# Convolution states and taps turned on the tensor engine, and an attention bias laid out by query in DRAM

## The chip, the cores and the metric

One core of a Trainium2 chip runs the whole kernel in one launch. The metric is the device time of one execution in microseconds (us). Three executions of the kernel before took 2809.85, 2809.88 and 2812.94 us; the median is 2809.88 us.

## The reference, cut to what matters

One layer of a streaming encoder is applied to 2048 prompt rows and 64 sample rows (2112 in all). Input LayerNorm is followed by one input projection, whose columns feed three head groups; their outputs go through an output projection, a LayerNorm, a convolutional feed-forward network and a last LayerNorm. Two pieces of it are touched here.

```
# band attention, per head: 128 queries see up to 640 keys
rel = arange(CHUNK)[:, None] + A_PAST_ROWS - arange(A_BAND)[None, :]
s = s + table[:, clip(rel, -63, 128) + 63]      # bias depends on query - key alone
# depthwise causal convolution of width 4 on the 896 x/B/C features
y = b + w[0]*xp[:, 0:L] + w[1]*xp[:, 1:1+L] + w[2]*xp[:, 2:2+L] + w[3]*xp[:, 3:3+L]
state_out = xp[:, L:]                            # last 3 rows, (3, 896), an output
```

The prompt starts from a zero state and the sample from `state_ssm_conv` (3, 896). Both end states are outputs: `prompt_ssm_conv` and `sample_ssm_conv`, each (3, 896). All numbers are float32; large products are made of three products of rounded high and low parts.

## The kernel before, in words

The kernel is seven stages, one after the other: `project_rows`, `project_features`, `attention`, `ssd_and_gmlp`, `mix_out`, `ffn_up`, `ffn_down`. A stage ends only when all its engines and all its stores are done, and the next one then begins on all engines together. Intermediate results pass through DRAM. Inside a stage each engine has its own instruction stream, and semaphores order them.

`project_features` (L375 to L667) computes q and k (6 tiles of 128 features) and the convolution's input (7 tiles, `NXBC`) with features on the partitions. It goes over the rows in seven groups of 304 (the last has 288); `step(g, p, i)` is one group, with 13 tiles j. TensorE (PE) writes tile j to PSUM bank j % 8; before tile j it waits until the tile four places before has been taken out (`evac_done`, L660). In the first group, eight tiles are accumulated side by side as the weights arrive. ScalarE (ACT) takes out q and k tiles (L544), after waiting for the store of the tile two before it in the same buffer; after the sixth it rounds the next group's input (`split_hi`, L536); then it takes out the convolution tiles (L566) and applies SiLU (L556). VectorE (DVE) makes the low parts (L600, L587) and the convolution (L613 to L631): `taps` and `shift` hold the filter with features on the partitions, `halo` and `halo_smp` the last three columns of the prompt and of the sample. SyncE (SP) loads weights (L453, L454) and issues the stores of q, k (L462, L463) and of the convolution (L467).

GpSimd (POOL) first issues eight loads (L487 to L491) for `taps`, `shift` and `halo_smp`. They turn (c, 896) rows into [128, 7] columns by moving one 4-byte element at a time. POOL then loads the second group's input (L484), spreads the bias table over 768 columns in `ext` on 6 partitions, stores it as `rel_ext` (L505), waits for that store, and only then loads the third group's input. At the end of the stage, SP stores the states with six more DMAs of 4-byte elements (L472, L474), and the stage waits for them (L475).

`attention` (L700 to L1048) starts with a load of `bias_up` on SP (L774), which reads `rel_ext` with overlapping rows, so that partition r holds the row that starts at column r. This is the bias with its query rows in reverse order. PE therefore multiplies it with a flipped identity, 12 matmuls in all (L962, L963), ACT copies the six results to `bias` (L939), and POOL writes the mask to two corners (L820, L821) and then issues eight loads of the key cache (L824) and three copies (L826 to L828). On SP, the load of the bias is followed by seven loads each for tiles 0 and 1 (L784, L787, L789) and, once all six heads of the tile before have been scored, for every later tile. Per head, PE computes scores (L979, L980), DVE adds the bias and takes the maximum (L861), ACT takes the exponential (L924), PE turns the result (L994) and multiplies with V (L1012). A tile is 128 queries, six heads; tile t sees min(t + 1, 5) blocks of keys.

```
sp.wait_ge(conv_done, NXBC * (NG + 1))                      # L470
for c in range(3):                                          # L471, again at L473 for the sample
    sp.dma_start(d["prompt_ssm_conv"][c].rearrange("(m p) -> p m", p=P), halo[:, :, c], ...)
pool.dma_start(d["rel_ext"], ext[:]).then_inc(ext_stored, 16)   # L505
pool.wait_ge(ext_stored, 16)                                    # L506
```

Of the kernel before, what the change touches and what calls it, by code (L numbers as in the profile page):

```python
# [33 lines left out]
HEADS = 6  # L34
# [340 lines left out]
def project_features(nc, d):  # L375
    with nc.cleanup_on_exit(), ExitStack() as ctx:
# [14 lines left out]
        halo, halo_smp = m.sb("halo", [P, NXBC, 3]), m.sb("halo_smp", [P, NXBC, 3])  # L391
        taps, shift = m.sb("taps", [P, NXBC, 4]), m.sb("shift", [P, NXBC])
        ext = m.sb("ext", [HEADS, WIN + P])
        ps_y = m.ps("ps_y", [P, 8, 512])
# [3 lines left out]
        small_loaded, halo_zeroed = m.sem("small_loaded"), m.sem("halo_zeroed")  # L398
# [43 lines left out]
        with nc.Block() as block:  # L442
            @block.sync
            def _(sp):
# [25 lines left out]
                sp.wait_ge(conv_done, NXBC * (NG + 1))  # L470
                for c in range(3):  # L471
                    sp.dma_start(d["prompt_ssm_conv"][c].rearrange("(m p) -> p m", p=P), halo[:, :, c], allow_slow_non_contiguous=True).then_inc(state_stored, 16)  # L472
                for c in range(3):  # L473
                    sp.dma_start(d["sample_ssm_conv"][c].rearrange("(m p) -> p m", p=P), halo_smp[:, :, c], allow_slow_non_contiguous=True).then_inc(state_stored, 16)  # L474
                sp.wait_ge(state_stored, 16 * 6)  # L475
# [5 lines left out]
            def _(pool):  # L481
# [4 lines left out]
                for c in range(4):  # L486
                    pool.dma_start(taps[:, :, c], d["ssm_conv_w"][c].rearrange("(m p) -> p m", p=P),  # L487
                                   allow_slow_non_contiguous=True).then_inc(small_loaded, 16)
                pool.dma_start(shift[:], d["ssm_conv_b"].rearrange("(m p) -> p m", p=P), allow_slow_non_contiguous=True).then_inc(small_loaded, 16)
                for c in range(3):  # L490
                    pool.dma_start(halo_smp[:, :, c], d["state_ssm_conv"][c].rearrange("(m p) -> p m", p=P),  # L491
                                   allow_slow_non_contiguous=True).then_inc(small_loaded, 16)
# [12 lines left out]
                pool.dma_start(d["rel_ext"], ext[:]).then_inc(ext_stored, 16)  # L505
# [16 lines left out]
            def _(act):  # L522
# [47 lines left out]
                groups(act, step)  # L570

            @block.vector
            def _(dve):
                for k in range(KD):
# [15 lines left out]
                dve.wait_ge(small_loaded, 128)  # L590
                dve.wait_ge(halo_zeroed, 1)

                def step(g, p, i):
# [11 lines left out]
                    for j in range(NXBC):  # L605
# [5 lines left out]
                        if tail(g):  # L611
                            dve.tensor_copy(c[:, TAIL + 3:TAIL + 6], halo_smp[:, j, :])
                        dve.tensor_copy(c[:, 0:3], halo[:, j, :]).then_inc(halo_in_done, 1)  # L613
# [5 lines left out]
                        dve.tensor_scalar(y, c[:, 0:nc_], taps[:, j, 0:1], shift[:, j:j + 1], ALU.mult,  # L619
                                          ALU.add).then_inc(tap_done, 1)  # L620
                        for e in (1, 2):
                            dve.wait_ge(tap_done, 3 * u + e)
                            dve.scalar_tensor_tensor(out=y, in0=c[:, e:e + nc_], scalar=taps[:, j, e:e + 1], in1=y,
                                                     op0=ALU.mult, op1=ALU.add).then_inc(tap_done, 1)
                        if tail(g):
                            dve.tensor_copy(halo_smp[:, j, :], c[:, n + 3:n + 6])
                            dve.tensor_copy(halo[:, j, :], c[:, TAIL:TAIL + 3])
                        else:
                            dve.tensor_copy(halo[:, j, :], c[:, n:n + 3])
                        dve.wait_ge(tap_done, 3 * u + 3)  # L630
                        dve.scalar_tensor_tensor(out=y, in0=c[:, 3:3 + nc_], scalar=taps[:, j, 3:4], in1=y,  # L631
# [4 lines left out]
            def _(pe):  # L636
                def step(g, p, i):
# [12 lines left out]
                    if first:  # L650

                        for k in range(KD):
# [3 lines left out]
                            for j in range(8):  # L656
                                product(j, k)
# [9 lines left out]
                groups(pe, step)  # L667

# [31 lines left out]
def attention(nc, d):  # L700


    with nc.cleanup_on_exit(), ExitStack() as ctx:
# [4 lines left out]
        bias, bias_up = m.sb("bias", [P, HEADS, WIN]), m.sb("bias_up", [P, HEADS, WIN])  # L708
        ident, flip, ident_r = m.sb("ident", [P, P]), m.sb("flip", [P, P]), m.sb("ident_r", [P, HD], F32R)
# [13 lines left out]
        flip_done, bias_flipped, bias_copied = m.sem("flip_done"), m.sem("bias_flipped"), m.sem("bias_copied")  # L723
# [45 lines left out]
        with nc.Block() as block:  # L769
            @block.sync  # L770
            def _(sp):

                toeplitz = bass.AP(d["rel_ext"].tensor, 0, [[1, P], [WIN + P, HEADS], [1, WIN]])
                sp.dma_start(bias_up[:], toeplitz).then_inc(bias_loaded, 16)  # L774
# [37 lines left out]
            def _(pool):  # L812
                make_identity(pool, ident, zero_done, ident_done)
                pool.memset(flip[:], 0.0).then_inc(zero_done, 1)
                pool.wait_ge(zero_done, 2)
                pool.affine_select(out=flip[:], in_=flip[:], compare_op=ALU.not_equal, fill=1.0, base=1 - P,
                                   pattern=[[1, P]], channel_multiplier=1).then_inc(flip_done, 1)

                pool.wait_ge(bias_copied, HEADS)
# [99 lines left out]
            def _(act):  # L919
# [17 lines left out]
                for h in range(HEADS):  # L937
                    act.wait_ge(bias_flipped, h + 1)
# [1648 lines left out]
```

## Time and profile before

| what | value |
|---|---|
| median of three runs | 2809.88 us |
| the profiled execution: its own time | 2820.15 us |
| the profiled execution: span of its instructions | 2818.7 us |
| mean granted clock of PE over the span | 0.957 of 2.4 GHz |
| busy: PE, DVE, ACT, POOL | 2577.7, 1638.2, 1053.8, 168.8 us |
| `project_features` | 291.7 to about 642 us of the span |
| `attention` | 642.5 to about 914 us of the span |

The profile is one execution. Its own time is 1.45 us above its span, and 10.27 us above the median of the runs. All positions below are microseconds from the start of its span. "Granted clock" is the share of the full 2.4 GHz that PE was given: 1.00, or 0.50 (1.2 GHz). The DMA share is the mean busy share of the 16 DMA engines; it can exceed 1 where transfers overlap. A landing time runs from the issue's start until the last byte has arrived. An entry like `[9.57 <-DMA at_v<-v_rows]` says how long the engine had been idle before this instruction, and what ended that.

### The profile page before, as it was taken

To read this page: it belongs to the slowest core of one execution; us is meant where nothing else is said; L and a number is where in the kernel's file an instruction comes from. 1 tells how busy PE (TensorE), PEld (TensorE's weight loads), DVE (VectorE), ACT (ScalarE), POOL (GpSimd) and SP (SyncE) were. 2 spreads that over 40 slices of the span, in tenths; PEclk is the share of its full clock that TensorE was granted. 3 is DMA by queue.
4 is the path that set the end of the run, shared out by engine and by line. 5 is a ranking of instruction groups with operands and counts; after the bars stand their busy time and mean duration, and the time that the engine had idled before them with its cause. 6 is when DMAs were issued, how large, how long until landed. Compare 5 with 4: busy or idle time off the path is not lost. (4 is left out here: it accounts for less than half of the span.)

```text
span 2818.7 us, 47061 instructions
## 1 busy us (share of the span) xinstructions
PE 2577.7 (91%) x15094; PEld 2363.7 (84%) x15094; DVE 1638.2 (58%) x3296; ACT 1053.8 (37%) x1996; POOL 168.8 (6%) x244
## 2 busy tenths in 40 slices
PE   6999799965998787995999989999999979999998
PEld 5888699964997776884899989999999967888885
DVE  5342445433775776665899986667766654333333
ACT  4444322214663113222555554445555442111110
POOL 0000100001000570110000000000000000000000
PEclk9999899987997898997999999999999989999999
DMA  5443623157441545444777779777788744322321
GB/s 198 137 156 118 207 97 101 66 50 176 118 126 38 169 140 199 161 159 155 256 245 245 243 252 292 257 258 250 239 257 255 245 165 145 94 77 78 93 78 52
DMA packets 418766, 468.52 MB, mean 166 GB/s; under 512 B 45309, under 2 KB 352389, under 8 KB 418651
## 3 DMA queue, kind: packets, MB, share of 16 engines
q1 hardware_dynamic: 405210, 418.50, 48.5%
q0 software_dynamic: 13456, 48.76, 5.2%
q8 instruction: 55, 0.90, 0.1%
q14 instruction: 45, 0.36, 0.0%
HBM read 312.51 MB, written 155.60 MB: 166 GB/s over the span
## 5 line engine op out<-in xcount | busy, mean ns | idle before, releaser
L2265 PE MATMUL fu_ps_a<-fu_x_hi,fu_w 128*128 128x354 f32 (+1 forms) x1056 | 348.2, 330 | 45.3 <-ACT fu_part L2042 16.9
L2267 PE MATMUL fu_ps_a<-fu_x_hi,fu_w 128*128 128x354 f32 (+1 forms) x1056 | 346.4, 328 | 0.0
L2266 PE MATMUL fu_ps_a<-fu_x_lo,fu_w 128*128 128x354 f32 (+1 forms) x1056 | 345.8, 328 | 0.0
L107 PE MATMUL fd_ps_y<-fd_w_hi,fd_h_hi 128*128 128x512 f32 (+1 forms) x748 | 292.5, 391 | 17.6 <-DVE fd_h_lo L2454 17.6
L108 PE MATMUL fd_ps_y<-fd_w_lo,fd_h_hi 128*128 128x512 f32 (+1 forms) x748 | 291.9, 390 | 0.0
L109 PE MATMUL fd_ps_y<-fd_w_hi,fd_h_lo 128*128 128x512 f32 (+1 forms) x748 | 291.6, 390 | 0.0
L2454 DVE TENSOR_TENSOR fd_h_lo<-fd_h_raw,fd_h_hi 128x256 fp32r<-128x256 f32 (+1 forms) x187 | 77.7, 417 | 311.6 <-ACT fd_h_hi L2426 311.6
L2265 PEld LDWEIGHTS fu_ps_a<-fu_x_hi,fu_w 128*128 128x128 f32 x1056 | 201.1, 190 | 53.5 <-ACT fu_part L2042 18.0
L107 PE MATMUL pf_ps_y<-pf_xt_hi,pf_w_hi 128*128 128x304 f32 (+1 forms) x728 | 221.2, 304 | 20.8 <-DVE pf_xt_lo L581 18.7
L2426 ACT CAST fd_h_hi<-fd_h_raw 128x256 fp32r<-128x256 f32 (+1 forms) x187 | 74.7, 401 | 404.8 <-PE fd_ps_y L109 394.2
L109 PE MATMUL pf_ps_y<-pf_xt_hi,pf_w_lo 128*128 128x304 f32 (+1 forms) x728 | 220.9, 303 | 0.0
L108 PE MATMUL pf_ps_y<-pf_xt_lo,pf_w_hi 128*128 128x304 f32 (+1 forms) x728 | 219.9, 302 | 0.0
L2266 PEld LDWEIGHTS fu_ps_a<-fu_x_lo,fu_w 128*128 128x128 f32 x1056 | 201.5, 191 | 0.0
L2267 PEld LDWEIGHTS fu_ps_a<-fu_x_hi,fu_w 128*128 128x128 f32 x1056 | 201.1, 190 | 0.0
L107 PEld LDWEIGHTS fd_ps_y<-fd_w_hi,fd_h_hi 128*128 128x128 f32 (+1 forms) x748 | 138.5, 185 | 51.2 <-DVE fd_w_lo L2492 16.8
L2265 PE MATMUL fu_ps_c<-fu_x_hi,fu_w 128*128 128x354 f32 (+1 forms) x528 | 174.5, 331 | 6.0 <-ACT fu_part L2061 6.0
L2266 PE MATMUL fu_ps_c<-fu_x_lo,fu_w 128*128 128x354 f32 (+1 forms) x528 | 173.3, 328 | 0.0
L2267 PE MATMUL fu_ps_c<-fu_x_hi,fu_w 128*128 128x354 f32 (+1 forms) x528 | 172.6, 327 | 0.0
L109 PEld LDWEIGHTS fd_ps_y<-fd_w_hi,fd_h_lo 128*128 128x128 f32 (+1 forms) x748 | 138.4, 185 | 32.0
L108 PEld LDWEIGHTS fd_ps_y<-fd_w_lo,fd_h_hi 128*128 128x128 f32 (+1 forms) x748 | 138.5, 185 | 31.6
L107 PEld LDWEIGHTS pf_ps_y<-pf_xt_hi,pf_w_hi 128*128 128x128 f32 x728 | 138.5, 190 | 21.4 <-DVE pf_xt_lo L581 18.9
L107 PE MATMUL pr_ps_y<-pr_w_hi,pr_xt_hi 128*128 128x512 f32 (+3 forms) x408 | 148.8, 365 | 4.7 <-DVE pr_xt_lo L306 4.7
(318 smaller groups left out, 5803.6 us busy)
## 6 DMA issues: line engine op xcount, KB each, us to landing
fu_w<-fu_w_split SPq DMA_DIRECT2D x176, 512.0 KB, 4.4
fu_w_raw<-ffn_w_in SPq DMA_DIRECT2D x132, 512.0 KB, 5.5
fu_w_split<-fu_w SPq DMA_DIRECT2D x44, 1024.0 KB, 4.6
fd_h_raw<-h_t SPq DMA_DIRECT2D x176, 128.0 KB, 2.2
h_t<-fu_val SPq DMA_DIRECT2D x88, 176.0 KB, 1.9
fd_raw<-ffn_w_out SPq DMA_DIRECT2D x22, 512.0 KB, 4.7
x_rows<-pr_xr SPq DMA_DIRECT2D x16, 512.0 KB, 2.8
xt<-pr_xt SPq DMA_DIRECT2D x16, 512.0 KB, 4.0
```

Source lines behind the costliest of these rows:

```text
L107: pe.matmul(out, lhs_hi, rhs_hi, start=first, stop=False)
L108: pe.matmul(out, lhs_hi, rhs_lo, start=False, stop=False)
L109: return pe.matmul(out, lhs_lo, rhs_hi, start=False, stop=last)
L2265: pe.matmul(out, wh, xh, start=first and k == 0, stop=False, skip_group_check=True)
L2266: pe.matmul(out, wh, xl, start=False, stop=False, skip_group_check=True)
L2267: last = pe.matmul(out, wl, xh, start=False, stop=k == KH - 1, skip_group_check=True)
L2426: act.copy(h_hi[:, x.slot, :, :x.n], h_raw[:, x.slot, :, :x.n]).then_inc(h_hi_done, 1)
L2454: dve.tensor_tensor(h_lo[:, x.slot, :, :x.n], h_raw[:, x.slot, :, :x.n], h_hi[:, x.slot, :, :x.n].bitcast(F32), ALU.subtract).then_inc(h_l ...
```

## The change

The eight small loads at the start of `project_features` become three, of contiguous 512-byte rows, into `vec_rows` (56 rows of 128); PE turns them in one transpose into PSUM bank 7, and DVE copies the result to `vecs` after the first low part. The six stores of the states become two PE transposes, two ACT copies and two stores of 21 rows of 512 bytes. `ext` is no longer stored once: POOL stores it 128 times over, shifted by one column each time, as `bias_rows` (6, 128, 640), 1920 KB, and still waits for this store. In `attention` ACT issues one load of `bias`, already in the right order, 768 rows of 2560 bytes; the flipped identity, the twelve matmuls and the six copies are gone. The layouts of `taps` and `halo` change with this.

```
 # project_features
+        ident, vec_rows, vecs = m.sb("ident", [P, P]), m.sb("vec_rows", [NV, P]), m.sb("vecs", [P, 8, NXBC])
+        taps, shift, halo_smp = vecs[:, 0:4], vecs[:, 4], vecs[:, 5:8]
+        halo, states_t = m.sb("halo", [P, 3, NXBC]), m.sb("states_t", [3 * NXBC, 2, P])
+        d["bias_rows"] = nc.dram_tensor("pf_bias_rows", (HEADS, P, WIN), F32, kind="Internal").ap()
...
 # SP
-                sp.wait_ge(conv_done, NXBC * (NG + 1))
-                for c in range(3):
-                    sp.dma_start(d["prompt_ssm_conv"][c]..., halo[:, :, c], ...).then_inc(state_stored, 16)
-                for c in range(3):
-                    sp.dma_start(d["sample_ssm_conv"][c]..., halo_smp[:, :, c], ...).then_inc(state_stored, 16)
-                sp.wait_ge(state_stored, 16 * 6)
+                sp.wait_ge(states_done, 2)
+                sp.dma_start(d["prompt_ssm_conv"].rearrange("c (m p) -> (c m) p", p=P), states_t[:, 0, :]).then_inc(state_stored, 16)
+                sp.dma_start(d["sample_ssm_conv"].rearrange("c (m p) -> (c m) p", p=P), states_t[:, 1, :]).then_inc(state_stored, 16)
+                sp.wait_ge(state_stored, 32)
 # POOL
-                for c in range(4): pool.dma_start(taps[:, :, c], ...)
-                pool.dma_start(shift[:], ...)
-                for c in range(3): pool.dma_start(halo_smp[:, :, c], ...)
+                pool.dma_start(vec_rows[0:4 * NXBC, :], ...).then_inc(vec_loaded, 16)
+                pool.dma_start(vec_rows[4 * NXBC:5 * NXBC, :], ...).then_inc(vec_loaded, 16)
+                pool.dma_start(vec_rows[5 * NXBC:, :], ...).then_inc(vec_loaded, 16)
+                make_identity(pool, ident, zero_done, ident_done)
...
-                pool.dma_start(d["rel_ext"], ext[:]).then_inc(ext_stored, 16)
+                by_query = bass.AP(ext[:].tensor, ext[:].offset + P - 1, [list(ext[:].ap[0]), [-1, P], [1, WIN]])
+                pool.dma_start(d["bias_rows"], by_query).then_inc(ext_stored, 16)
                 pool.wait_ge(ext_stored, 16)
 # ACT, after the last group
+                act.wait_ge(states_turned, 1)
+                for e in range(2):
+                    act.copy(states_t[:, e, :], ps_y[0:3 * NXBC, 7, e * P:(e + 1) * P]).then_inc(states_done, 1)
 # DVE, after the first low parts
+                    if k == 0:
+                        dve.wait_ge(vec_turned, 1)
+                        dve.tensor_copy(vecs[:].rearrange("p a b -> p (a b)"), ps_y[:, 7, 0:NV]).then_inc(vec_done, 1)
 # PE, before the first group, before tile 7 of it, and after the last group
+                pe.wait_ge(ident_done, 1)
+                pe.wait_ge(vec_loaded, 48)
+                pe.transpose(ps_y[:, 7, 0:NV], vec_rows[:], ident[0:NV, 0:NV]).then_inc(vec_turned, 1)
...
+                                if k == 0 and j == 7:
+                                    pe.wait_ge(vec_done, 1)
...
+                pe.wait_ge(conv_done, NXBC * (NG + 1))
+                for e, rows in enumerate((halo[:]..., halo_smp...)):
+                    last = pe.transpose(ps_y[0:3 * NXBC, 7, e * P:(e + 1) * P], rows, ident[:])
+                last.then_inc(states_turned, 1)
 # attention: SP, POOL, ACT, PE
-                toeplitz = bass.AP(d["rel_ext"].tensor, 0, [[1, P], [WIN + P, HEADS], [1, WIN]])
-                sp.dma_start(bias_up[:], toeplitz).then_inc(bias_loaded, 16)
-                pool.memset(flip[:], 0.0) ... pool.affine_select(out=flip[:], ...)
-                pool.wait_ge(bias_copied, HEADS)
+                pool.wait_ge(ident_done, 1)
+                pool.wait_ge(bias_loaded, 16)
                 pool.memset(bias[0:64, :, WIN - 64:], MASKED)
                 pool.memset(bias[64:P, :, 0:64], MASKED).then_inc(bias_done, 1)
-                for h in range(HEADS):
-                    act.wait_ge(bias_flipped, h + 1)
-                    act.copy(bias[:, h, :], (ps_s[:, 0] if h % 2 == 0 else ps_t)[:, 0:WIN]).then_inc(bias_copied, 1)
+                act.dma_start(bias[:], d["bias_rows"].rearrange("h p c -> p h c")).then_inc(bias_loaded, 16)
-                pe.wait_ge(flip_done, 1)
-                pe.wait_ge(bias_loaded, 16)
-                for h in range(HEADS):
-                    ...
-                    pe.matmul(dst[:, 0:512], flip[:], bias_up[:, h, 0:512], start=True, stop=True)
-                    pe.matmul(dst[:, 512:WIN], flip[:], bias_up[:, h, 512:], start=True, stop=True).then_inc(bias_flipped, 1)
-                pe.wait_ge(bias_copied, HEADS)
```

## Rows read from the trace of the kernel before

**Rows 1.** the page: busy time and share of each engine over the span.

```profile
PE 2577.7 (91%) x15094; PEld 2363.7 (84%) x15094; DVE 1638.2 (58%) x3296; ACT 1053.8 (37%) x1996; POOL 168.8 (6%) x244
```

**Rows 2.** the stretch view; columns: sum, engines, granted clock, DMA share, GB/s.

```profile
620.00:630.00 10.00, 0.00 (x0) 0.00 (x0) 0.00 (x0) 0.00 (x0) 0.00 (x0) 0.50 1.96 1
```

**Rows 3.** the timeline from the last convolution to the first attention instructions.

```profile
612.70 0.52 DVE L631 SCALAR_TENSOR_TENSOR pf_conv<-pf_cin,pf_taps,pf_conv 128x291 f32<-128x291 f32 x1
616.06 4.59 SPq L474 DMA_DIRECT2D sample_ssm_conv<-pf_halo_smp  x3
...
642.54 0.37 SPq L774 DMA_DIRECT2D at_bias_up<-rel_ext  x1
```

**Rows 4.** the view by tile, pf_halo_smp: issues, and time to landing.

```profile
L474 SPq DMA_DIRECT2D sample_ssm_conv<-pf_halo_smp x3: 563/567/3371, 616.1 to 617.3; - x3
...
DMA to landing us min/median/max: 6.6/13.4/24.2
```

**Rows 5.** nearest rows for the operations that are new (three views).

```profile
L994 PE MATMUL at_ps_t<-at_ident,at_s x450: 216/273/435, 662.8 to 898.9; 128*128 128x128 f32 x140, 64*128 64x64 f32 x8, 64*64 64x64 f32 x2
...
607.33 0.22 ACT L564 COPY pf_cin<-pf_ps_y 128x64 f32<-128x64 f32 x1
...
dt_rows<-pr_dt_out SPq DMA_DIRECT2D x16, 3.0 KB, 1.6
```

**Rows 6.** the timeline at the start of attention.

```profile
650.44 1.12 SPq L789 DMA_DIRECT2D at_v<-v_rows  x1
...
660.64 0.33 PE L979 MATMUL at_ps_s<-at_k_hi,at_q 128*128 128x128 f32 x1 [0.78 <-ACT at_bias L939]
...
661.69 0.29 DVE L861 CUSTOM_DVE_ANT_0 at_s<-at_ps_s,at_bias 128x128 f32<-128x128 f32 x1 [18.27 <-POOL at_bias L821]
...
681.76 0.69 PE L979 MATMUL at_ps_s<-at_k_hi,at_q 128*128 128x384 f32 x1 [9.57 <-DMA at_v<-v_rows]
```

**Rows 7.** landing times: the bias load; V of tile 0; V of all tiles (L789).

```profile
at_bias_up<-rel_ext SPq DMA_DIRECT2D x1, 1920.0 KB, 8.4
...
DMA to landing us min/median/max: 6.4/6.4/6.4
...
DMA to landing us min/median/max: 2.7/4.0/12.5
```

**Rows 8.** the stretch view at the start of attention (columns as in Rows 2).

```profile
651.00:652.00 1.00, 0.91 (x1) 0.50 (x2) 0.00 (x0) 0.00 (x0) 0.00 (x0) 0.50 1.23 227
662.00:663.00 1.00, 0.68 (x5) 0.54 (x5) 0.91 (x7) 0.79 (x4) 1.00 (x2) 1.00 0.00 0
```

**Rows 9.** the start of the projection: the small loads, the first split and product.

```profile
L487 POOL DMA_DIRECT2D pf_taps<-ssm_conv_w x4: 982/990/1023, 292.2 to 295.2; - x4
...
299.00 1.21 ACT L529 CAST pf_xt_hi<-pf_xt 128x1216 fp32r<-128x1216 f32 x1 [1.38 <-DMA pf_xt<-xt]
...
301.72 0.62 PE L107 MATMUL pf_ps_y<-pf_xt_hi,pf_w_hi 128*128 128x304 f32 x1 [18.69 <-DVE pf_xt_lo L581]
```

**Rows 10.** the stretch view there.

```profile
300.00:306.00 6.00, 4.28 (x17) 4.29 (x18) 1.77 (x2) 1.78 (x2) 0.24 (x2) 0.50 1.00 234
306.00:316.00 10.00, 10.00 (x69) 9.88 (x69) 7.21 (x5) 5.91 (x5) 0.00 (x0) 0.95 1.04 395
```

**Rows 11.** around the table's store: POOL, ACT, and two DMAs' landings.

```profile
331.14 0.54 POOL L505 DMA_DIRECT2D rel_ext<-pf_ext  x1 [0.30 <-POOL pf_ext L503]
...
335.17 0.42 ACT L544 ACTIVATE pf_qk_hi<-pf_ps_y 128x304 fp32r<-128x304 f32 x1 [1.92 <-DMA qk_lo<-pf_qk_lo]
...
DMA to landing us min/median/max: 5.8/6.3/6.7
...
pf_xt<-xt POOLq DMA_DIRECT2D x5, 1216.0 KB, 7.0
```

**Rows 12.** ACT in the second group of the projection.

```profile
372.27 2.22 ACT L536 CAST pf_xt_hi<-pf_xt 128x2432 fp32r<-128x2432 f32 x1
...
388.64 0.41 ACT L566 COPY pf_cin<-pf_ps_y 128x304 f32<-128x304 f32 x1 [1.98 <-PE pf_ps_y L109]
```

More of the change, by code:

```diff
@@ L484, in load_xt @@
                     pool.dma_start(xt[:, p, :, :n], d["xt"][:, :, gcols(g)]).then_inc(xt_loaded[p], 16)
[L486 to L492, printed above, removed]
+                pool.dma_start(vec_rows[0:4 * NXBC, :], d["ssm_conv_w"].rearrange("c (m p) -> (c m) p", p=P)).then_inc(vec_loaded, 16)
+                pool.dma_start(vec_rows[4 * NXBC:5 * NXBC, :], d["ssm_conv_b"].rearrange("(m p) -> m p", p=P)).then_inc(vec_loaded, 16)
+                pool.dma_start(vec_rows[5 * NXBC:, :], d["state_ssm_conv"].rearrange("c (m p) -> (c m) p", p=P)).then_inc(vec_loaded, 16)
+                make_identity(pool, ident, zero_done, ident_done)
                 pool.memset(halo[:], 0.0).then_inc(halo_zeroed, 1)
@@ L588, in split_lo @@
                                       ALU.subtract).then_inc(xt_lo_done, 1)
-                dve.wait_ge(small_loaded, 128)
+                dve.wait_ge(vec_done, 1)
                 dve.wait_ge(halo_zeroed, 1)
@@ L622, in step @@
                             dve.wait_ge(tap_done, 3 * u + e)
-                            dve.scalar_tensor_tensor(out=y, in0=c[:, e:e + nc_], scalar=taps[:, j, e:e + 1], in1=y,
+                            dve.scalar_tensor_tensor(out=y, in0=c[:, e:e + nc_], scalar=taps[:, e, j:j + 1], in1=y,
                                                      op0=ALU.mult, op1=ALU.add).then_inc(tap_done, 1)
                         if tail(g):
-                            dve.tensor_copy(halo_smp[:, j, :], c[:, n + 3:n + 6])
-                            dve.tensor_copy(halo[:, j, :], c[:, TAIL:TAIL + 3])
+                            dve.tensor_copy(halo_smp[:, :, j], c[:, n + 3:n + 6])
+                            dve.tensor_copy(halo[:, :, j], c[:, TAIL:TAIL + 3])
                         else:
-                            dve.tensor_copy(halo[:, j, :], c[:, n:n + 3])
+                            dve.tensor_copy(halo[:, :, j], c[:, n:n + 3])
                         dve.wait_ge(tap_done, 3 * u + 3)
-                        dve.scalar_tensor_tensor(out=y, in0=c[:, 3:3 + nc_], scalar=taps[:, j, 3:4], in1=y,
+                        dve.scalar_tensor_tensor(out=y, in0=c[:, 3:3 + nc_], scalar=taps[:, 3, j:j + 1], in1=y,
                                                  op0=ALU.mult, op1=ALU.add).then_inc(conv_done, 1)
@@ L667, in _ @@
                 groups(pe, step)
+                pe.wait_ge(conv_done, NXBC * (NG + 1))
+                for e, rows in enumerate((halo[:].rearrange("p a b -> p (a b)"), halo_smp.rearrange("p a b -> p (a b)"))):
+                    last = pe.transpose(ps_y[0:3 * NXBC, 7, e * P:(e + 1) * P], rows, ident[:])
+                last.then_inc(states_turned, 1)
 class Band:
@@ L707, in attention @@
         cache = m.sb("cache", [P, 4, HEADS, 2, HD])
-        bias, bias_up = m.sb("bias", [P, HEADS, WIN]), m.sb("bias_up", [P, HEADS, WIN])
-        ident, flip, ident_r = m.sb("ident", [P, P]), m.sb("flip", [P, P]), m.sb("ident_r", [P, HD], F32R)
+        bias = m.sb("bias", [P, HEADS, WIN])
+        ident, ident_r = m.sb("ident", [P, P]), m.sb("ident_r", [P, HD], F32R)
         s = m.sb("s", [P, 3, WIN])
```

22 lines of the change are left out of this document (7 added, 15 removed).

## The prediction

> **What bounds the kernel now.** I read the page first: PE is busy in 91% of the span [rows 1], so a change elsewhere counts only where PE has nothing to do. The stretch view shows such a place: from 620 to 630 us no engine works, the DMA engines show a share of 1.96 and move 1 GB/s [rows 2]. The timeline says what that is. The last convolution starts at 612.70 and takes 0.52 us; then SP issues six stores of 4-byte elements, and the next stage starts at 642.54 [rows 3]. The view by tile gives the last of these: issued at 617.3, it lands up to 24.2 us later, at 641.5 [rows 4]. So 29.3 us lie between the last convolution (613.2) and attention, and the next stage starts 1.05 us after that landing. The third place is attention's own start. PE's first score starts at 660.64 after a wait for the copies of the turned bias, the first bias is added at 661.69, and later PE stands 9.57 us, until 681.76, for the values of tile 2 [rows 6]. I call attention's start S (642.54 now). The last two places are in the projection: its first product at 301.72 waits for a chain that begins with the input's landing at 299.0 [rows 9], and PE meets late stores near 335 [rows 11].
>
> **The change part by part.**
>
> 1. *States at the end of the projection.* Removed are six stores and their landing. Added, one after the other: two turns on PE, at 0.27 us each and at most 0.44 [rows 5], about 0.6 us with their start; two ACT copies of 128 columns, a little over the 0.22 us for 64 columns [rows 5], 0.5 us; two issues on SP of some 0.5 us, and the landing, 1.6 us for the smallest store [rows 5]. That is 613.2 + 0.1 + 0.6 + 0.1 + 0.5 + 0.1 + 0.6 (the second issue starts) + 1.8 = 617.0; with a margin for the waits 617.4, and S comes 1.05 later, at 618.4. Gain 24.1 us; bounds 21 (each store lands in 5 us) and 25. PE has just come out of full clock, so its two turns may run at half clock; the 0.44 covers that.
>
> 2. *Filter and states at the start.* POOL issues three loads of 56 rows instead of eight of 7168 elements, each of which occupied it for 0.98 us or more [rows 9]. From 300 to 306 us the DMA engines were as busy as later (1.00 against 1.04) but moved 234 GB/s against 395 [rows 10]; the small loads are what differs. The first weights and half of the input must land before ACT can start at 299.00 [rows 9]: at the higher rate some 1.3 us earlier, after which ACT's own first cast is in the way. Against it PE now waits for the three loads and a turn. The last of them is issued near 294.3 and lands 2 to 6 us later, and the turn (0.3 to 0.44) lies before the first split is ready at about 300.3 or just behind it. DVE's copy (0.2 us) falls in its idle time, and PE needs it only at the eighth tile, some 5 us in. POOL's identity, 0.5 us, is behind its loads and ahead of nothing that is late. I take a gain of 1.0; bounds a loss of 1 and a gain of 1.5.
>
> 3. *The table's store.* POOL's store at 331.14 [rows 11] grows from 18 KB to 1920 KB, in 768 rows of 2560 bytes read from 6 partitions, and POOL still waits for it. No row shows such a store. The nearest is the load of the same 768 rows on 128 partitions, which lands in 8.4 us [rows 7]. If six engines carry it at the share that one of 16 had there (1920 KB in some 6.4 us is 19 KB per us and engine), 320 KB each take 17 us, so 18 to 19 with landing. I take 18 us. It hits two things. First, the stores of q and k tiles in flight at 333 to 340. Beside the next input's load these landed in 5.8 to 6.7 us, and ACT waited for such a store at 335.17 already [rows 11]. Now the ones before them are late as well, by 3 to 4 us, of which PE (four banks ahead) passes on about 2; with the late convolution stores after it I count 3.5. Second, the third group's input is loaded after it, 7.0 us [rows 11]. In the second group ACT splits that input at 372.27 (2.22 us) and cannot take out a convolution tile before; PE's twelfth tile needs that one and would start when the eleventh is done, at 388.6 [rows 12]. So the store may take 388.6 - 331.1 - 7.3 - 2.6 = 47 us before PE waits, and each us beyond costs one. At 18 it costs nothing. Loss 3.5; bounds 1 and 12.
>
> 4. *The bias in attention.* SP's own load goes (0.4 us), ACT issues the new one, and POOL's flip, PE's 12 matmuls and ACT's six copies go, a chain of about 9 us behind the bias's landing. Yet the time does not fall by that. Tile 0's V was issued at 650.44 and landed 6.4 us later [rows 6, 7], at S + 14.3, and tile 1's loads were behind it; the DMA engines ran at 1.23 with 225 GB/s in that stretch and only at 662 stood still [rows 8]. The same 1920 KB and the same tiles must still come in. So the first score moves from S + 18.1 to about S + 14, a gain of 4 there, and the next wait is again for loads: POOL's cache loads, behind the mask, start at about S + 11 instead of S + 18.9 and now meet tile 1's loads. What sets the end is tile 2's V, which landed at S + 39.2 (681.76) [rows 6]. Its loads are preceded by the same bytes and gain only the DMA engines' idle time at 662 and their weaker stretch after it, in all 2 to 3.5 us. I take 3.0; bounds 0 and 5, and a loss of 3 if the order turns bad. PE idles and cools before tile 2 either way. Afterwards nothing in attention or behind it is touched.
>
> *Sum*, against the profiled execution's 2820.15 us: 24.1 + 1.0 - 3.5 + 3.0 = 24.6, so 2795.5 us. The median of the runs lies 10.27 us below that execution, so the forecast is 2785.3 us.
>
> **The rivals.**
>
> *A, the table's store is far slower* (about 50 us instead of 18), because six partitions cannot be read as fast as 128. For it: 1920 KB come out of 6 partitions; against it: nothing measured. The third group's input then comes 3 us too late, and for some 45 us every store of the projection that shares an engine with it lands late, another 5 us beyond my 3.5. Gain 24.6 - 8 = 16.6: 2793.3 us.
>
> The Trainium skill (SBUF — State Buffer, section "Door 1: The DMA port swizzle") puts partitions 0 to 3 on one port of some 27 GB/s; four of the six rows of `ext` would then take about 48 us. No row of this trace reads so much from so few partitions, so none shows it.
>
> *B, attention gives nothing back*: the early cache loads (eight on POOL) delay tiles 1 and 2, and tile 2's values land 1 us later after S than now. For it: landing rose from a median of 4.0 to 12.5 us when they met tile 2's loads [rows 7]. Gain 24.1 + 1.0 - 3.5 - 1 = 20.6: 2789.3 us.
>
> *C, slower than before.* The table's store runs through one engine. At 19 KB per us it takes about 100 us; the third group's input, the split and the convolution copy behind it come 53 us after PE's eleventh tile: 24.6 - 53 is a loss of 28.4, 2838.3 us. It breaks even at 47 + 24.6 = 72 us of store, and is measurably slower from 78. Against it: the bias load of as many rows was spread over the engines [rows 7, 8].
>
> *D, the states are not what the stage waits for.* Then S would hardly move and only parts 2 to 4 count, about 2809 us. Against it: no other transfer is in flight, 1 GB/s is moved, and the next stage follows the last landing by 1.05 us [rows 2 to 4].
>
> **How the numbers follow.** Forecast 0.50, A 0.28, B 0.13, C 0.04, D 0.02, and 0.03 for a store between A and C that about cancels the gain. The range starts at 2779, where part 1 gives 25, part 2 1.5, part 3 costs 1 and part 4 gives 5 (2779.4), and reaches through B and A, with A's own spread, to 2797. A measurement of this kernel can tell 0.2% (5.6 us) from no change: above 2815.5 is only C (0.04), within lie D and half of the last case (0.04), and faster holds 0.92.
>
> **What would show it.** In the profile after: attention starts 5 us after the last convolution, not 29; both state stores land in about 2 us; PE's first projection product comes near 300.7; POOL's wait for the table's store (18 us, or 50) stands before its load of the third group's input; ACT's second split near 372 waits for DMA only in A and C; in attention the first score comes near S + 14 and the first of tile 2 near S + 36. The forecast is wrong if the table's store lasts over 47 us, if stores of the projection land in more than 8 us for long, or if tile 2 starts later than S + 39.

## The result, and the profile after

The changed kernel took 2832.17 us, median of four runs (2828.67 to 2835.51); the kernel before, beside it, 2810.02 us (2809.85 to 2812.94). The ratio is 1.0073, 95% interval 1.0054 to 1.0091: slower by 22 us, where 2785.3 us was forecast. The profiled execution of after has 2828.87 us of its own and a span of 2827.4 us. The last convolution now ends at 661.6 instead of 613.2. The whole loss arises before that point; what follows it is faster than before.

The page of after, busy time and share by engine, as in [rows 1]:

```profile
PE 2560.0 (91%) x15073; PEld 2350.3 (83%) x15073; DVE 1638.8 (58%) x3297; ACT 1049.4 (37%) x1992; POOL 163.2 (6%) x239
```

PE has 18 us less to do than before (for the most part the flips, and the stretch at half clock told of at the end), so the loss is idle time. The view of PE's waits names it. Its columns are who waits for what, total us, times, longest us; the window runs from the projection to attention's start.

```profile
PE pf_ps_y L107 <- ACT pf_qk_hi L545: 50.1, 1, 50.1
PE at_ps_s L979 <- DMA at_v<-v_rows: 17.5, 1, 17.5
PE pf_ps_y L646 <- DMA pf_vec_rows<-state_ssm_conv: 15.4, 1, 15.4
PE pf_ps_y L683 <- DVE pf_conv L638: 3.1, 1, 3.1
```

50.1 us stand in one wait of the projection, for ACT's take-out of a q/k tile; before, this wait was 2.1 us. It is new, and it is the first thing to follow back. The timeline from 326 to 381 us, of POOL, then ACT, then PE:

```profile
326.40 1.10 POOL L506 DMA_DIRECT2D pf_bias_rows<-pf_ext  x1 [0.30 <-POOL pf_ext L503]
385.37 0.93 POOL L487 DMA_DIRECT2D pf_xt<-xt  x1 [57.88 <-DMA pf_bias_rows<-pf_ext]
...
363.95 0.42 ACT L545 ACTIVATE pf_qk_hi<-pf_ps_y 128x304 fp32r<-128x304 f32 x1 [35.27 <-DMA qk_lo<-pf_qk_lo]
380.37 0.42 ACT L545 ACTIVATE pf_qk_hi<-pf_ps_y 128x304 fp32r<-128x304 f32 x1 [15.99 <-DMA qk_lo<-pf_qk_lo]
...
380.84 0.62 PE L107 MATMUL pf_ps_y<-pf_xt_hi,pf_w_hi 128*128 128x304 f32 x1 [50.15 <-ACT pf_qk_hi L545]
```

The landing times of the table's store and of the new bias load:

```profile
pf_bias_rows<-pf_ext POOLq DMA_DIRECT2D x1, 1920.0 KB, 58.4
at_bias<-pf_bias_rows ACTq DMA_DIRECT2D x1, 1920.0 KB, 9.0
```

POOL's store lasts 58.4 us, not 18. ACT needs a free `qk_lo` buffer for the next tile and stands 35.27 and then 15.99 us for SP's stores of the tiles before. The view by tile of `pf_qk_lo` from 326 to 390 us has those stores:

```profile
L468 SPq DMA_DIRECT2D qk_lo<-pf_qk_lo x6: 434/3204/6739, 329.4 to 387.4; - x6
...
DMA to landing us min/median/max: 4.0/13.3/38.8
```

They land in up to 38.8 us. In [rows 11] ACT waited 1.92 us for such a store. The stretch view (columns as in [rows 2]) says that this is no lack of bandwidth overall: from 340 to 380 us almost nothing computes, and the DMA engines move 40 to 61 GB/s at a share of 0.28 to 0.38. A share of 0.38 of 16 engines is six of them. Six rows of `ext` are being stored. Why the share is lower after 360 us is told with experiments 5 to 7.

```profile
300.00:306.00 6.00, 4.82 (x19) 4.82 (x20) 5.03 (x4) 3.17 (x2) 0.00 (x0) 0.50 1.04 398
340.00:360.00 20.00, 0.00 (x0) 0.00 (x0) 0.00 (x0) 0.00 (x0) 0.00 (x0) 0.50 0.38 61
360.00:380.00 20.00, 0.00 (x0) 0.00 (x0) 0.47 (x1) 0.42 (x1) 0.00 (x0) 0.50 0.28 40
```

The three other places. The end of the projection and attention's start, all engines, answering to [rows 3]:

```profile
661.11 0.52 DVE L638 SCALAR_TENSOR_TENSOR pf_conv<-pf_cin,pf_vecs,pf_conv 128x291 f32<-128x291 f32 x1
661.69 0.29 PE L683 MATMUL pf_ps_y<-pf_ident,pf_halo 128*21 128x128 f32 x1 [3.10 <-DVE pf_conv L638]
662.17 0.39 ACT L574 COPY pf_states_t<-pf_ps_y 21x128 f32<-21x128 f32 x2
662.72 0.37 SPq L476 DMA_DIRECT2D prompt_ssm_conv<-pf_states_t  x1
663.14 0.28 SPq L477 DMA_DIRECT2D sample_ssm_conv<-pf_states_t  x1
...
665.49 0.72 SPq L798 DMA_DIRECT2D at_q<-qk_hi  x1
```

From the end of the last convolution (661.63) to S (665.49) it is 3.86 us, not 29.3. PE's first score, and its next wait in attention, answering to [rows 6]:

```profile
679.57 0.45 PE L979 MATMUL at_ps_s<-at_k_hi,at_q 128*128 128x128 f32 x1 [17.48 <-DMA at_v<-v_rows]
695.08 0.58 PE L979 MATMUL at_ps_s<-at_k_hi,at_q 128*128 128x256 f32 x1 [9.98 <-DMA at_v<-v_rows]
```

The start of the projection, answering to [rows 9]:

```profile
297.89 1.89 DVE L580 TENSOR_TENSOR pf_w_lo<-pf_w_raw,pf_w_hi 128x1664 fp32r<-128x1664 f32 x1 [11.52 <-ACT pf_w_hi L526]
298.57 0.32 PE L646 MATMUL pf_ps_y<-pf_ident,pf_vec_rows 56*128 56x56 f32 x1 [15.42 <-DMA pf_vec_rows<-state_ssm_conv]
299.70 1.42 DVE L585 TENSOR_TENSOR pf_xt_lo<-pf_xt,pf_xt_hi 128x1216 fp32r<-128x1216 f32 x1
301.18 0.29 PEld L107 LDWEIGHTS pf_ps_y<-pf_xt_hi,pf_w_hi 128*128 128x128 f32 x1 [2.46 <-DVE pf_xt_lo L585]
```

### The profile page after: what moved, and what is told of

Read it like the earlier page. It is cut to its first block and busy times, and to the rows that moved or that the text cites. A ratio compares the mean times of both kernels' runs of the same rounds, so it can differ in the third digit from the quotient of the medians.

```text
span 2827.4 us, 47008 instructions
## 1 busy us (share of the span) xinstructions
PE 2560.0 (91%) x15073; PEld 2350.3 (83%) x15073; DVE 1638.8 (58%) x3297; ACT 1049.4 (37%) x1992; POOL 163.2 (6%) x239
## 3 DMA queue, kind: packets, MB, share of 16 engines
q0 software_dynamic: 14304, 50.71, 5.8%
## 5 line engine op out<-in xcount | busy, mean ns | idle before, releaser
L107 PE MATMUL pf_ps_y<-pf_xt_hi,pf_w_hi 128*128 128x304 f32 (+1 forms) x728 | 221.9, 305 | 52.4 <-ACT pf_qk_hi L545 50.1
```

The lines of the kernel that those rows point to most:

```text
L107: pe.matmul(out, lhs_hi, rhs_hi, start=first, stop=False)
```

## The experiments

Fifteen kernels were run. "Ratio" is against the kernel before on the same chip, whose median was between 2812.8 and 2817.9 us there, with the 95% interval. S is attention's start in the profile.

**1. The states alone, with the filter.** The change's projection, but the 18 KB store of the table and attention as before.

```diff
-                pool.dma_start(d["bias_rows"], by_query).then_inc(ext_stored, 16)
+                pool.dma_start(d["rel_ext"], ext[:]).then_inc(ext_stored, 16)
```

> The states and the filter are turned on PE as in the change; the table's store (18 KB) and the whole attention are those of before. Theory 1 (the stored table costs about 50 us, the states and the filter give about 25): 2810 - 25.5 - 0.5 = about 2784 us, attention starts 4 us after the last convolution, no PE wait beyond 2.2 us in the projection's first group. Rival (the states' gain is taken back by attention's start, where the loads then are late): 2795 us or more.

Measured: 2791.29 us, ratio 0.9918 (0.9894 to 0.9942). S came at 619.8, not 642.5. So parts 1 and 2 together keep about what they promised, and the loss is in the table's store. The time is above the expected 2784 us, though, and one wait is longer than the 2.2 us expected. POOL, ACT and PE near 330 us in this kernel:

```profile
328.55 0.94 POOL L487 DMA_DIRECT2D pf_xt<-xt  x1 [2.01 <-DMA rel_ext<-pf_ext]
...
335.00 0.42 ACT L544 ACTIVATE pf_qk_hi<-pf_ps_y 128x304 fp32r<-128x304 f32 x1 [4.47 <-DMA qk_lo<-pf_qk_lo]
335.48 0.62 PE L107 MATMUL pf_ps_y<-pf_xt_hi,pf_w_hi 128*128 128x304 f32 x1 [5.98 <-ACT pf_qk_hi L544]
```

**2. The bias alone.** The kernel before with the large store, and the change's attention.

```diff
-                pool.dma_start(d["rel_ext"], ext[:]).then_inc(ext_stored, 16)
+                pool.dma_start(d["bias_rows"], by_query).then_inc(ext_stored, 16)
```

> The bias by query alone: the projection stores 1920 KB from 6 partitions and attention loads it, while states and filter move in 4-byte elements as before. Theory 1: the change's 2829 to 2835 us plus the 26 us of the states and the filter, 2855 to 2861 us. Rival (the turn on PE at the start or the new layout of the halo has a share in the loss): less than 2850 us.

Measured: 2856.94 us, ratio 1.0147 (1.0116 to 1.0178). The store lands in 58.4 us again, and PE waits 42.5 us for ACT's q/k tiles. The loss belongs to this half of the change, whatever the other half does.

**3. Is it POOL's wait?** As after, but POOL does not wait for the store before it loads the third group's input.

```diff
                 pool.dma_start(d["bias_rows"], by_query).then_inc(ext_stored, 16)
-                pool.wait_ge(ext_stored, 16)
...
                 step(NG - 2, 0, NG // 2 - 1)
+                pool.wait_ge(ext_stored, 16)
```

> As the change, but GpSimd does not wait for the table's store before it loads the third group's input; it waits at the end of its stream. Theory 1 (the cost is that the q and k stores queue behind the table's rows on shared DMA engines): nothing gained, PE still waits 45 to 50 us in the first group, 2826 to 2836 us. Rival, the way in which the prediction thought that a slow store would cost (the third group's input comes late): the time falls by 10 us or more.

Measured: 2836.24 us, ratio 1.0061 (1.0042 to 1.0079). The input is issued 58 us earlier, and nothing is gained: ACT still waits 37.59 us for a store of `qk_lo`. POOL and ACT:

```profile
327.67 0.93 POOL L487 DMA_DIRECT2D pf_xt<-xt  x1
...
365.80 0.42 ACT L545 ACTIVATE pf_qk_hi<-pf_ps_y 128x304 fp32r<-128x304 f32 x1 [37.59 <-DMA qk_lo<-pf_qk_lo]
```

So the path over which I had let the store cost anything large, the third group's input, carries none of it.

**4. Another place.** The same store, issued behind POOL's other work, at 470 us.

```diff
-                pool.dma_start(d["bias_rows"], by_query).then_inc(ext_stored, 16)
-                pool.wait_ge(ext_stored, 16)
...
                 step(NG - 2, 0, NG // 2 - 1)
+                pool.dma_start(d["bias_rows"], by_query).then_inc(ext_stored, 16)
+                pool.wait_ge(ext_stored, 16)
```

> As the change, but the same slow store of the table is issued at the end of GpSimd's stream, in the fifth or sixth group, where a q or k tile comes every 3.3 us. Theory 1: with two buffers per store each tile tolerates a landing of some 6 us, the table's rows make it 10 to 39 us, so PE still waits 30 to 50 us there: 2810 to 2835 us. Rival (only the first group is that tight, its eight tiles coming at once): 2790 us or less.

Measured: 2821.25 us, ratio 1.0011 (0.9997 to 1.0025), ten runs. The store still takes 58.6 us. These are PE's waits in the projection, of which one (5.4 us, at 337 us) lies in the first group, long before the store:

```profile
PE pf_ps_y L107 <- ACT pf_qk_hi L545: 17.7, 2, 12.3
PE pf_ps_y L107 <- ACT pf_cin L567: 11.3, 2, 8.2
```

So PE waits 23.6 us beside the store, in three waits, instead of 50.1; the expected 30 to 50 us were too much. ACT stands there for stores of the convolution (11.4, 9.8, 12.3, 9.5 and 6.6 us) more than for those of q and k. The place is worth some 17 us by the ratios; in neither place is the slow store free.

**5 to 7. Why the store is slow.** Three kernels change only where the table's rows are read from. Twice `ext` keeps its rows further apart (two and four partitions); once the 18 KB store is followed by a copy of 1920 KB from DRAM to DRAM, so that no partition is read.

```diff
-        ext = m.sb("ext", [HEADS, WIN + P])
+        ext = m.sb("ext", [4 * HEADS, WIN + P])      # the rows used: 0, 4, ..., 20
...
-                by_query = bass.AP(..., [list(ext[:].ap[0]), [-1, P], [1, WIN]])
+                by_query = bass.AP(..., [[4 * ext[:].ap[0][0], HEADS], [-1, P], [1, WIN]])
```

```diff
+                by_query = bass.AP(d["rel_ext"].tensor, P - 1, [[WIN + P, HEADS], [-1, P], [1, WIN]])
+                pool.dma_start(d["bias_rows"], by_query).then_inc(ext_stored, 16)
```

> As the change, but the six rows of the table lie on partitions 0, 4, 8, 12, 16 and 20 instead of 0 to 5; the same bytes, rows and descriptors. Theory 1 (reading is slow because neighbouring partitions share one way out of SBUF): the store lands in about 15 to 20 us instead of 58, PE's wait in the first group falls from 50 to 5 to 12 us, the time to 2786 to 2796 us. Theory 2 (six engines carry it, whatever the source): 58 us and 2829 us or more, as the change.

> As the change, but the table's rows lie on partitions 0, 2, 4, 6, 8 and 10. In the change four rows lay in the first four partitions (58.4 us), with rows four apart one did (19.4 us). Theory 1: two rows share the way out of each four partitions, so the store takes about half of 58.4 us, 27 to 32 us, PE waits 18 to 27 us in the first group, and the time is 2798 to 2808 us. Rival (any distance is as good as four): 19 to 20 us and about 2793 us.

> As the change, but the 18 KB table is stored to DRAM first and the 1920 KB are then copied from there, in the same order by head, on the same queue and at the same place. Theory 1 (slow only because they come out of neighbouring partitions): 12 to 22 us instead of 58, and 2785 to 2797 us. Rival (the long store costs by its destination, or by the order of its rows): about 58 us and 2829 us or more.

Landing times of the 1920 KB, with rows four apart, two apart, and out of DRAM:

```profile
pf_bias_rows<-pf_ext POOLq DMA_DIRECT2D x1, 1920.0 KB, 19.4
```

```profile
pf_bias_rows<-pf_ext POOLq DMA_DIRECT2D x1, 1920.0 KB, 32.6
```

```profile
pf_bias_rows<-rel_ext POOLq DMA_DIRECT2D x1, 1920.0 KB, 19.2
```

| rows read from | store, us | PE's wait for q/k tiles, us | time, us | ratio |
|---|---|---|---|---|
| partitions 0 to 5 (after) | 58.4 | 50.1 | 2832.17 | 1.0073 (1.0054 to 1.0091) |
| 0, 2, ..., 10 | 32.6 | 24.5 | 2809.97 | 0.9964 (0.9951 to 0.9976) |
| 0, 4, ..., 20 | 19.4 | 13.1 | 2792.65 | 0.9923 (0.9901 to 0.9946) |
| DRAM | 19.2 | 8.1 | 2788.16 | 0.9905 (0.9874 to 0.9935) |

PE's wait in the third of these kernels:

```profile
PE pf_ps_y L107 <- ACT pf_qk_hi L548: 13.1, 1, 13.1
```

In the first three rows of the table nothing changes but the distance of the source rows (and that `ext` is cleared beforehand where they are apart), and the duration falls with the number of rows among four neighbouring partitions: four, two, one. With one it equals the copy that reads no partition, so there something else limits. PE's wait falls with it, and stays 6 to 11 us below the store's length. With the rows two apart the time is 2 us above the expected range, with the rows four apart the wait is 1 us above it.

The three durations alone would also fit groups of eight partitions roughly, in which six, four and two rows lie (58.4 us would then become 39 and 19). The stretch view of after speaks for groups of four:

```profile
351.00:357.00 6.00, 0.00 (x0) 0.00 (x0) 0.00 (x0) 0.00 (x0) 0.00 (x0) 0.50 0.39 60
357.00:363.00 6.00, 0.00 (x0) 0.00 (x0) 0.00 (x0) 0.00 (x0) 0.00 (x0) 0.50 0.25 30
372.00:378.00 6.00, 0.00 (x0) 0.00 (x0) 0.00 (x0) 0.00 (x0) 0.00 (x0) 0.50 0.24 27
```

Until 357 us six of the 16 DMA engines are busy (0.39), from then on four (0.25). 357 us is 31 us after the issue, about as long as the store with two rows in each group took (32.6): the two rows on partitions 4 and 5 are through, the four on partitions 0 to 3 are not. In the last stretch those four move 27 GB/s together.

**8. Fewer bytes.** `ext` is stored 16 times, shifted by eight columns (243 KB), and the bias comes in eight loads of 240 KB.

```diff
+                by_eight = bass.AP(..., ext[:].offset + P - 8, [list(ext[:].ap[0]), [-8, 16], [1, WIN + 7]])
+                pool.dma_start(d["bias_part"], by_eight).then_inc(ext_stored, 16)
...
+                for b in range(8):
+                    act.dma_start(bias[b:P:8], d["bias_part"][:, :, 7 - b:7 - b + WIN]...)
```

> As the change, but the table is stored 16 times instead of 128 times over (shifted by eight columns each time, 243 KB from the same 6 partitions), and attention loads the bias with eight DMAs of 240 KB on ACT's queue. Theory 1: the store lands in 58.4 / 8 = about 7 to 9 us, PE waits some 3 to 6 us in the first group, and the time is 2782 to 2788 us. A theory by which the store's bytes do not matter (something else in the projection costs the 50 us) leaves it near 2829 us. If eight issues make the bias late in attention, its first score comes later than S + 15.

Measured: 2796.79 us, ratio 0.9935 (0.9915 to 0.9956). The store takes 9.0 us, PE's wait for q/k tiles is 8.4 us, but the first score comes only at S + 18.4: eight issues stand in ACT's stream and the loads compete with tile 0's. That is 9 us above the expected range. It repairs the store and gives part of it back in attention; that the issues and the loads are what delays the score was not tested apart.

**9, 10. Parts 1 and 2 apart.** The end states alone turned on PE; then the filter and the start states alone. The rest is as before in both.

```diff
 # states alone: ident built as in the change; loads of taps, shift, halo_smp as before
+                    last = pe.transpose(ps_y[0:3 * NXBC, 7, e * P:(e + 1) * P], rows, ident[:])
 # filter alone: the six element-wise state stores as before
+                pe.transpose(ps_y[:, 7, 0:NV], vec_rows[:], ident[0:NV, 0:NV]).then_inc(vec_turned, 1)
```

> Only the end states are turned on PE; the filter comes in 4-byte elements and attention is that of before. Expected: attention starts 3.9 us after the last convolution instead of 29.3, so 25.4 us less, PE's wait in the first group stays at 2 us: ratio to before 0.991. If the gain is partly taken back by attention, the ratio is above 0.993.

> Only the filter and start states come as rows and are turned on PE; the end states are stored in 4-byte elements and attention is that of before. Theory (the weights then come earlier and take the third group's input load with them into the first q and k stores): PE's first product 0.5 to 1.1 us earlier, its wait in the first group 5 to 7 us against 2.1, the last convolution 2 to 4 us later, 0.1% slower than before. The prediction's part 2 said 1.0 us faster.

Measured: states alone 2789.40 us, ratio 0.9907 (0.9889 to 0.9926), S at 617.8. Filter alone 2818.72 us, ratio 1.0015 (1.0003 to 1.0027), S at 646.4. POOL's load of the third group's input and PE's wait, states alone:

```profile
334.60 0.94 POOL L487 DMA_DIRECT2D pf_xt<-xt  x1 [2.00 <-DMA rel_ext<-pf_ext]
...
333.66 0.41 PE L107 MATMUL pf_ps_y<-pf_xt_hi,pf_w_hi 128*128 128x304 f32 x1 [2.10 <-ACT pf_qk_hi L548]
```

The same, filter alone:

```profile
329.20 0.94 POOL L489 DMA_DIRECT2D pf_xt<-xt  x1 [2.01 <-DMA rel_ext<-pf_ext]
...
337.83 0.62 PE L107 MATMUL pf_ps_y<-pf_xt_hi,pf_w_hi 128*128 128x304 f32 x1 [6.82 <-ACT pf_qk_hi L546]
```

The states carry the whole gain. The ratios of the three parts alone (states, filter, and the bias of experiment 2) multiply to 1.0068, and the whole change has 1.0073. The filter's part loses 4 us, with an interval that just excludes no change. Its input load is issued 5.4 us before that of the states alone, and PE's wait is 4.7 us longer.

**11. Order restored.** To a kernel like experiment 1 (with the cache loads of experiment 12) POOL's wait for the first six low parts is added before the third group's input.

```diff
+                pool.wait_ge(qk_lo_done, NQK)
                 def step(g, p, i):
```

> States and filter as in the change, attention as before with the late cache loads, and GpSimd issues the third group's input only when the first six q and k tiles are out. Without that wait the input's load starts at 329 us, meets the first q and k stores, and PE waits 7.3 us in the first group (2.1 before the change). Expected: PE waits 1 to 2.5 us, last convolution 4 to 6 us earlier, 2782 to 2784 us against 2787.8 on another chip. Rival: the wait has another cause and stays above 5 us.

Measured: 2784.17 us, ratio 0.988 (0.9858 to 0.9902); PE's wait is 2.1 us again, 7.3 without the edit, and S comes at 615.2 instead of 621.6. The intervals of the two ratios overlap, so the wait shows the effect and the time doesn't resolve it.

**12 to 14. Attention's loads, and the late store of far rows.** The eight cache loads and three copies are issued behind tile 3's output instead of at attention's start: once in experiment 1's kernel, once in a kernel with the change's attention, rows four apart and the store at the end of POOL's stream. That kernel is also run without this edit (the second text below).

```diff
                         store_o(before, 1 - p)
+                        if isinstance(before.t, int) and before.t == 3:
+                            load_caches()
```

> States and filter as in the change, attention as before, but the eight cache loads and three copies of attention are issued only after tile 3 is stored. If they are what makes tile 2's V late, PE's wait of 8 us for it falls below 3 us and the time is 4 to 8 us less than that of the same kernel with the early loads (2791.3 us on that chip). Rival: tile 2's loads are late by themselves, the wait stays.

> As the change, but the table's rows on partitions 0, 4, ... 20 and their store at the end of GpSimd's stream. If 19 us of store at a place without the first group's rush hide behind PE, PE does not wait and the gain over the far rows at their old place is 8 to 11 us (2792.7 us there). If the two buffers of q and k are the limit wherever it is put, PE still waits 5 to 13 us.

> As the far rows stored at the end of GpSimd's stream (2787.35 us on another chip), and attention's cache loads and three copies issued only after tile 3. There PE waited 29.3 us in all for V of tiles 0 to 2, 17.7 of them for tile 0, which no cache load can touch. If the rest (11.6 us) comes from the cache loads, it falls below 4 us and the time is 2777 to 2782 us. Rival: the waits are set by the bias load, which shares the engines, and stay.

| kernel | time, us | ratio | attention, us |
|---|---|---|---|
| old bias, cache early (experiment 1) | 2791.29 | 0.9918 (0.9894 to 0.9942) | 262.5 |
| old bias, cache late | 2787.78 | 0.9891 (0.9873 to 0.991) | 256.7 |
| new bias, cache early | 2787.35 | 0.9891 (0.9869 to 0.9913) | 260.3 |
| new bias, cache late | 2775.37 | 0.9845 (0.9823 to 0.9866) | 253.6 |

Attention is counted from S to the next stage's first instruction. The new bias is worth 2.2 us (cache early) and 3.1 us (cache late) in these profiles, the late cache loads some 6 us. Only with the new bias are the late loads clear of noise in the time; with the old one the intervals overlap, but PE's wait for tile 2's values falls from 8.2 to 2.3 us.

The third kernel of the table also says something of the store. With rows four apart and the store late, the 1920 KB take 21.0 us, and PE has no wait beside them: its only wait for ACT, 5.0 us, is at 336 us, in the first group. At that place a store of 21 us costs nothing that the profile shows, where one of 58.6 us (experiment 4) costs 23.6 and one of 19.4 us in the first group stands beside a wait of 13.1.

**15. All together.** New bias, rows four apart, store at the end of POOL's stream, late cache loads, POOL's wait for the low parts.

> All that helped: states and filter turned on PE, the table's rows four partitions apart and stored at the end of GpSimd's stream, attention's cache loads late, and the third group's input only after the first six q and k tiles. Against the same without the last wait (2775.4 us, PE waits 5.2 us in the first group): PE waits 1 to 2.5 us, and the time is 2770 to 2773 us, ratio to before 0.983 or less.

Measured: 2772.37 us (2769.80 to 2775.67), ratio 0.9851 (0.9828 to 0.9875), better than both kernels; the version before it, in the last line of the table, is equal within the intervals, and the expected ratio of 0.983 or less was missed. The table's store of this kernel lands in 20.9 us:

```profile
pf_bias_rows<-pf_ext POOLq DMA_DIRECT2D x1, 1920.0 KB, 20.9
```

PE's waits of this kernel from the projection on, total us, times, longest us, with the two that matter:

```profile
PE at_ps_s L987 <- DMA at_v<-v_rows: 19.4, 2, 17.9
PE pf_ps_y L107 <- ACT pf_qk_hi L550: 2.1, 1, 2.1
```

What remains at attention's start is a wait of 17.9 us for the values of tile 0.

## Why the prediction was wrong, point by point

*Part 1, the states: right.* Forecast 24.1 us, bounds 21 to 25. From the last convolution's end to S it is 29.3 - 3.9 = 25.4 us less, and alone the part moves S by 24.7. The chain of turns, copies and two small stores was as worked out. Rival D is refuted by the same row.

*Part 2, filter and start states: wrong in sign.* I had counted 1.0 us gained. PE's first product came 0.5 us earlier (301.18): ACT splits the input 0.8 us earlier (298.20 instead of 299.00), and 0.3 us of that is lost because DVE, still busy with `w_lo` (from 297.89), starts the input's low part at 299.70. The moved bandwidth was there: 398 GB/s from 300 to 306 us, against 234 in [rows 10]. What the step left out is the other end of POOL's stream: with the small loads gone, the load of the third group's input is issued at 328.55 instead of 333.94 (experiment 1), its 1216 KB meet the first stores of q and k, and PE waits 6.0 to 7.3 us instead of 2.1. Experiment 10 shows the net loss, experiment 11 that the order is the cause of the longer wait. In after it is buried under the table's store.

*Part 3, the table's store: this is the step that failed*, and in two terms. The length: I took 18 us from the load of the same rows into 128 partitions [rows 7], at one engine's share each. That is what a copy from DRAM or from rows four apart takes (19.2 and 19.4 us). From six neighbouring partitions it took 58.4. Rival A had this length, and the reason that the prediction gave it. The Trainium skill (SBUF — State Buffer, section "Door 1: The DMA port swizzle") puts partitions 0 to 3 on one port. By that rule four, two and one of the rows share a port in the three kernels. The runs agree: 58.4, 32.6 and 19.4 us. By its 27 GB/s the estimate in the prediction was 48 us. In the stretch from 372 to 378 us the trace agrees with that figure: 27 GB/s for the four rows of one port. Over the whole 58.4 us the 4 x 320 KB are 22 GB/s; where the missing 10 us go is not shown.

The price: I had let q and k stores be late by 3 to 4 us, and the main cost come by the third group's input, free up to 47 us of store. Rival A's 8 us were worked out in the same way, so the right length there still gave 2793.3 us. Measured are 50.1 - 2.1 = 48.0 us, by the path that I had priced at 2. While six of the 16 DMA engines carry the table, SP's stores of q and k land in up to 38.8 us, which I read as their using engines of that set too; `qk_lo` has two buffers, so ACT stops after two tiles, and PE once its four banks are full. My "forecast is wrong if" line named this sign (stores landing in more than 8 us for long), but the sum did not use it: in the first group, with buffers two deep, a store that others are held up by costs nearly its whole length. The shorter stores had shorter waits there (58.4, 32.6 and 19.4 us of store, 50.1, 24.5 and 13.1 us of wait). At 470 us the same store costs 23.6 us, and one of 21 us nothing, so the place counts as well; why it does stays open. That it is shared engines and not a shared queue rests on the share of 0.38 and on the two queues being different ones (in the pages, q0 grows from 48.76 to 50.71 MB with the table, and SP's stores are in q1); no run shows how one engine shares its time between two queues.

*Rival C* had the sign and, with 2838.3 us, nearly the time, but by another mechanism: no engine took the table alone, and the split it put the loss on is not where PE stands. The kernel is slower at 58 us of store, while C needed 78.

*Part 4, attention: right in size.* Forecast: first score at about S + 14, 3.0 us gained. Measured: 679.57, that is S + 14.1, and 2.2 to 3.1 us between kernels that differ in the bias (262.5 in experiment 1 against 259.8 in after makes 2.7). The first product of tile 2 starts at 701.80, S + 36.3, where about S + 36 was forecast. Attention in the profile of before took 272.1 us, but 8.5 us of that went with a stretch below full clock, told of at the end, and not with the bias. Experiment 15's attention against experiment 11's, 250.9 against 256.2, makes 5.3, so single profiles leave it between 2 and 5 us. The order turned otherwise than I had written, though: PE's next long wait, 9.98 us, is for tile 1's values, and tile 2 has none. The cache loads cost about 6 us there, with the old bias as with the new, so rival B's collision is real but no news of this change.

*The sum*: 25.4 + 0.5 + 2.7 - 48.0 = -19.4, a loss of 19.4 us. From before's median, 2810.0, that leads to 2829.4 us; the median of after is 2832.17. The remaining 2.8 us are in none of these terms.

## What to carry to other kernels

Before a store is enlarged, look at which partitions it reads, not only at its bytes: 1920 KB out of six neighbouring rows took 58 us, and 19 us with the rows four apart. Then list who else stores in that time and how many buffers lie between such a store and the bound engine; with two buffers and tiles coming close together, nearly the whole length came through, and at another place of the same stage a store of 21 us cost nothing. And when loads at the head of a queue are removed, follow the queue to its next large load: what moves forward can land among transfers that it used to miss.

## What was unexpected of the hardware

Profile against profile the two kernels differ by 8.72 us, median against median by 22. The profiled execution of before is 10 us slower than its median, and a stretch of attention in it accounts for most of that. The stretch view of the kernel before, columns as in [rows 2]:

```profile
857.50:862.50 5.00, 5.00 (x23) 4.81 (x23) 1.86 (x6) 1.40 (x3) 0.54 (x1) 0.50 0.11 43
862.50:867.50 5.00, 5.00 (x21) 4.71 (x21) 2.31 (x8) 1.40 (x3) 0.00 (x0) 0.50 0.00 2
```

PE works without a gap here and is granted 0.50, that is 1.2 GHz; before it, from 842.5 to 852.5, it was busy for 4.33 and 2.74 us of each five at 1.00. The four slices from 852.5 to 872.5 have 0.57, 0.50, 0.50 and 0.72, some 8.5 us of full-clock work lost. At the same place of the program, behind the same half-busy stretch, experiment 1 kept 1.00 throughout, the states-alone kernel had 0.58, 0.50 and 0.55 for 15 us, and after had one slice at 0.66. The four profiles with the old bias and early cache loads have 272.1 us of attention (before), 269.2 (states alone), 268.0 (filter alone) and 262.5 (experiment 1); less the full-clock work lost in their slices, 8.5, 6.9, 5.2 and 0 us, they lie between 262.3 and 263.6. So this drop comes in some executions and not in others, and a single profile of this kernel is uncertain by about its size. What decides whether it comes is not shown.
